# Turning TensorE's partial rows with a 0/1 matrix instead of the identity, in a two-layer hybrid block on one core

## The reference, cut to what matters

```
silu_c, silu_cc = silu(c), silu(c_ctx)
for l in range(2):
    mod_l = (silu_c @ ada_w[l] + ada_b[l]).reshape(6, 1024)     # ada_w[l] is 1024 x 6144
    mod_c = (silu_cc @ ada_w[l] + ada_b[l]).reshape(6, 1024)
    sh1, sc1, g1, sh2, sc2, g2 = mod                            # for each of the two streams
    h = rmsnorm(x, norm_mix_g[l]) * (1 + sc1) + sh1
    y = mixer(h)                   # l = 0: RG-LRU and a 31-tap convolution; l = 1: attention
    x = x + g1 * y
    h = rmsnorm(x, norm_ffn_g[l]) * (1 + sc2) + sh2
    scores = sigmoid(h @ router_w)                              # router_w is 1024 x 16
    sel = scores + router_bias     # best group of 4 experts, then the top 2 inside it
    x = x + g2 * (sum over the chosen experts of gate * expert(h))
return rmsnorm(x_latent, final_norm_g)
```

## Time and profile before

| | |
|---|---|
| runs (3) | 1002.47 us median, 1002.4 to 1004.44 |
| the profiled execution | 1001.4 us |
| its span in the profile | 999.6 us |
| TensorE busy | 906.7 us, 91% of the span |
| TensorE weight loads | 473.6 us |
| VectorE busy | 379.8 us, 38% |
| ScalarE busy | 255.3 us, 26% |
| GpSimd busy | 112.9 us, 11% |
| read from and written to HBM | 314 GB/s over the span |

### The profile page before, as it was taken

One profiled execution on the slowest core, in us unless ns is written; L12 is line 12 of the kernel. 1 busy time (PEld: TensorE's weight loads), 2 busy tenths in 40 slices (PEclk: granted clock), 3 DMA queues, 4 the chain that ended last, 5 costly groups with the idle time before them and its releaser, 6 DMA issues.

```text
span 999.6 us, 14180 instructions
## 1 busy us (share of the span) xinstructions
PE 906.7 (91%) x5142; PEld 473.6 (47%) x5143; DVE 379.8 (38%) x815; ACT 255.3 (26%) x393; POOL 112.9 (11%) x220
## 2 busy tenths in 40 slices
PE   3899999999689999999999869999959999998786
PEld 1433343444346655665656434467424455554443
DVE  1389989833542222222222261774351111111012
ACT  3423446412312111112211230264121111111112
POOL 2300000100021111111111210000003111111010
PEclk9999999999989999999999969999978999999999
DMA  9992595756699899999999983971577999999994
GB/s 352 348 350 84 200 340 217 275 210 253 242 376 330 324 396 379 399 395 396 396 395 400 360 292 128 368 284 49 205 263 252 379 389 395 391 396 392 395 391 191
DMA packets 133652, 314.32 MB, mean 314 GB/s; under 512 B 4516, under 2 KB 4884, under 8 KB 133616
## 3 DMA queue, kind: packets, MB, share of 16 engines
q1 hardware_dynamic: 120144, 275.78, 74.5%
q0 software_dynamic: 8800, 29.75, 8.2%
q10 hardware_dynamic: 4672, 8.30, 2.3%
HBM read 299.35 MB, written 14.47 MB: 314 GB/s over the span
## 4 chain that ended last, share of the span: by engine, by line
PE 61%; DMA 27%; DVE 6%; ACT 3%; issue 2%; POOL 0%; ACTq 0%; SPq 0%; DVEq 0%; POOLq 0%
PE ps L757 17%; PE ps L770 9%; PE ps L559 8%; PE ps L595 6%; DMA weight_ring<-in_exp_w_up 6%; DMA weight_ring<-in_exp_w_down 5%; DMA weight_ring<-in_exp_w_gate 4%; PE ps L828 3%; PE ps L488 3%; PE ps L870 3%; DMA arena<-in_exp_w_up 2%; DMA hT<-in_exp_w_down 2%; DMA arena<-in_exp_w_gate 2%; DMA weight_ring<-in_ev_w_in 2%; DVE arena L1059 2%
## 5 line engine op out<-in xcount | busy, mean ns | idle before, releaser
L757 PE MATMUL ps<-weight_ring,arena 128*64 128x256 f32 x1792 | 201.4, 382 | 10.7 <-DMA weight_ring<-in_exp_w_up 5.6
L757 PEld LDWEIGHTS ps<-weight_ring,arena 128*64 128x64 f32 x1792 | 140.5, 138 | 79.0 <-issue 19.6
L1330 DVE TENSOR_TENSOR arena<-arena,ps 128x128 f32<-128x128 f32 x78 | 18.9, 284 | 269.0 <-PE ps L757 269.0
L559 PE MATMUL ps<-hT,weight_ring 128*128 128x512 f32 x256 | 113.6, 597 | 1.1 <-DMA weight_ring<-in_ev_w_in 0.6
L770 PE MATMUL ps<-weight_ring,arena 128*64 128x512 f32 x448 | 102.3, 597 | 2.5 <-DVE arena L1343 0.2
L1059 DVE SCALAR_TENSOR_TENSOR arena<-arena,par 128x512 f32<-128x512 f32 x132 | 95.0, 749 | 5.3 <-PE ps L559 1.2
L757 PE MATMUL ps<-arena 128*64 128x256 f32 x704 | 80.1, 385 | 5.1 <-DMA arena<-in_exp_w_up 4.8
L1713 ACT ACT_TABLE_LOAD x39 | 50.0, 1283 | 129.5 <-issue 129.2
L559 PEld LDWEIGHTS ps<-hT,weight_ring 128*128 128x128 f32 x256 | 47.4, 190 | 64.4 <-issue 63.0
L757 PEld LDWEIGHTS ps<-arena 128*64 128x64 f32 x704 | 56.6, 139 | 31.5 <-issue 6.1
L595 PE MATMUL ps<-weight_ring,arena 128*128 128x512 f32 x160 | 70.8, 595 | 0.7 <-DVE arena L1480 0.5
(11 more groups left out here) (315 smaller groups left out, 906.1 us busy)
## 6 DMA issues: line engine op xcount, KB each, us to landing
weight_ring<-in_ada_w SPq DMA_DIRECT2D x24, 2048.0 KB, 12.7
weight_ring<-in_exp_w_gate SPq DMA_DIRECT2D x22, 2048.0 KB, 10.8
weight_ring<-in_exp_w_up SPq DMA_DIRECT2D x22, 2048.0 KB, 12.0
weight_ring<-in_exp_w_down SPq DMA_DIRECT2D x22, 2048.0 KB, 11.8
arena<-in_exp_w_gate SPq DMA_DIRECT2D x10, 2048.0 KB, 11.2
hT<-in_exp_w_down SPq DMA_DIRECT2D x10, 2048.0 KB, 11.8
arena<-in_exp_w_up SPq DMA_DIRECT2D x10, 2048.0 KB, 12.0
weight_ring<-in_ev_w_in SPq DMA_DIRECT2D x4, 2048.0 KB, 19.2
```

The source lines that it names most:

```text
L559: last = mm(ps[:, m % 4, :], wide(slot)[:, k, P * j:P * j + P], hT[:, k, :], start=(k == 0), stop=(k == KD - 1))
L757: last = mm(ps[64 * fh:64 * fh + 64, bank, 0:256], xgT[:, k % 4, 64 * (k // 4):64 * (k // 4) + 64], w[:, k, 256 * fh:256 * fh + 256], star ...
```

## The change

The turn is no longer a transpose. The partial tile stays the stationary operand, but what moves past it is `sel`: the product of the turned tile with `sel` adds the four partial rows at once. For the modulation two columns of `sel` are used, for the router 16. VectorE's reduction of a chunk becomes an addition of the bias while it is read from PSUM, and the later `add_bias` is gone; the waits that it held stay. The router's reduction is gone, and ScalarE's sigmoid reads the logits from PSUM.

```diff
-        s_ls = sem("logits_summed")
...
 def ada_columns(bank=7):
...
                 for i in range(4):
-                    last = tr(ps[:, bank, P * i:P * i + P], ada_part[:, n % 2, P * i:P * i + P], ident[:, :])
+                    last = mm(ps[:, bank, 2 * i:2 * i + 2], ada_part[:, n % 2, P * i:P * i + P], sel[:, 0:2], start=True, stop=True)
                 last.then_inc(s_col, 1)
...
 def logits(i0, i1, count):
...
                     for i in range(i0, i1):
-                        last = tr(ps[:, 7, P * i:P * i + P], ada_part[:, 0, P * i:P * i + P], ident[:, :])
+                        last = mm(ps[:, 7, E * i:E * i + E], ada_part[:, 0, P * i:P * i + P], sel[:, :], start=True, stop=True)
                     last.then_inc(s_lg[l], 1)
...
 def sum_columns(count, bank=7):
...
-                    v.tensor_reduce(mods[:, l, 4 * c:4 * c + 4, :],
-                                    ps[:, bank, :].rearrange("p (i g m) -> p i m g", i=4, g=4)[:, :, 0:2, :], AX,
-                                    ALU.add).then_inc(s_red, 1)
-
-            def add_bias(l, c0, c1):
-
-                dve.wait_ge(s_red, ada[0])
-                w = mods[:, l, 4 * c0:4 * c1, :]
-                b0 = C_ADAB + 48 * l
-                return v.tensor_tensor(w, w, par[:, b0 + 4 * c0:b0 + 4 * c1].unsqueeze(2).to_broadcast([P, 4 * (c1 - c0), 2]),
-                                       ALU.add)
+                    b0 = C_ADAB + 48 * l + 4 * c
+                    v.tensor_tensor(mods[:, l, 4 * c:4 * c + 4, :], ps[:, bank, 0:8].rearrange("p (i m) -> p i m", i=4),
+                                    par[:, b0:b0 + 4].unsqueeze(2).to_broadcast([P, 4, 2]), ALU.add).then_inc(s_red, 1)
 
             sum_columns(4)
-            link(add_bias(0, 0, 4))
+            dve.wait_ge(s_red, ada[0])
...
                     if ada[0] == 10:
-                        link(add_bias(0, 4, 10))
+                        dve.wait_ge(s_red, ada[0])
...
-                dve.wait_ge(s_lg[l], 2)
-                v.tensor_reduce(logit_sb(l).rearrange("p (t e) -> p t e", t=n),
-                                ps[:, 7, 0:P * n].rearrange("p (t g m) -> p t m g", t=n, g=4)[:, :, 0:E, :], AX,
-                                ALU.add).then_inc(s_ls, 1)
                 dve.wait_ge(s_sc, l + 1)
...
-                act.wait_ge(s_ls, l + 1)
-                s.activation(score_sb(l), logit_sb(l), ACT.Sigmoid).then_inc(s_sc, 1)
+                act.wait_ge(s_lg[l], 2)
+                s.activation(score_sb(l), ps[:, 7, 0:E * n], ACT.Sigmoid).then_inc(s_sc, 1)
```

More of the change, by code:

```diff
@@ L337, in score_sb @@
             return rt(l, (848, 984)[l], 64)[:, 0:E * len(toks(l))]
-        def logit_sb(l):
-            return rt(l, (912, 1048)[l], 64)[:, 0:E * len(toks(l))]
         OH_GATE = 3600
@@ L1179, in _ @@
             add_residual(0, range(NT), lambda t: 0 if cond_of(t) == CON else 1, after_residual)
-            link(add_bias(0, 10, 12))
+            dve.wait_ge(s_red, ada[0])
             dve.sem_inc(s_mods, 1)
@@ L1298, in route @@
                     sum_columns(1, 3)
-                    link(add_bias(1, 10, 12))
+                    dve.wait_ge(s_red, ada[0])
                     dve.sem_inc(s_mods, 1)
@@ L1311, in route @@
                     sum_columns(1, 3)
-                    link(add_bias(1, 0, 6))
+                    dve.wait_ge(s_red, ada[0])
                     dve.sem_inc(s_mods, 1)
@@ L1388, in _ @@
                     sum_columns(1)
-            link(add_bias(1, 6, 10))
+            dve.wait_ge(s_red, ada[0])
             link(gain(mods[:, 1, 8 * SC2:8 * SC2 + 8, :], 1, SC2, C_FFNG + 8))
```

## The result

The change makes the kernel slower: 1016.26 us (median of 6 runs, 1011.49 to 1018.05) against 1002.43 (6 runs, 1000.59 to 1004.44) beside it, a ratio of 1.0132 [1.0117, 1.0147]. The profiled execution took 1017.79, its span is 1016.0, 16.4 more than before.

What follows compares the result with a forecast made beforehand. It took TensorE (61% of the chain) and transfers (27%) as the bound. Terms 0.9 + 2.4 + 1.7 - 0.44 + 0.65 - 0.36 + 0.1 = +4.95 us on 1002.47 gave 1007.4, range 1004.2 to 1010.3.

Steps and rivals of the forecast that it cites:

- The turn: Each chunk's turn on TensorE: eight passes taking 0.86 instead of 0.43, so +0.43 us each.
- L704's step: 0.107 us between float32 passes at L704, with 34 moving columns; taken to hold for the turn's 2 columns.
- Small passes are cheap: Rival: passes step on after 0.027, a turn saves 0.21, -3.3 in all, 999.2 us; chance 8%.
- Passes don't overlap: Rival: each pass waits for the one before, +1.8 a turn on some 14 turns, +25, 1027 us; chance 3%.
- Head stage: From 52.9 to 192: longer turns ahead of the steps VectorE waits for, +2.4 us.
- output projection: Up to 258: four longer turns on a TensorE queue that nothing else holds up, +1.7 us.
- projection between the MoEs: Two turns in the projection count, two fall in TensorE's gap before the expert rows; +0.65 us.
- Start: Up to 52.9: four longer turns in series make L559 1.4 to 1.8 late, +0.9 us after waiting time there.
- the transfer at 52.9: Awaited weight chunk that stays in place; 0.57 of waiting and about 0.17 of drain there cover part of the start's delay.
- First and second router: Sigmoid reads PSUM and starts earlier, -0.44 and -0.36 us; a late turn in the second adds +0.1.
- just inside that wait: First router: two turns growing by 0.85 and 0.43 fit the first MoE tile's 1.21 wait; otherwise the gain is lost.
- TensorE slows down: Rival: nearly empty passes in full-rate stretches bring on 1.2 GHz; one or two falls of 1.9, 1009.3 to 1011.2; chance 10%.

Runs made afterwards that it cites:

- head_out_new: Kernel before, with the new turns only for chunks 4 to 14 (head stage and output projection); 1006.26 us, ratio 1.0054 to before.
- start_ident_product: Kernel before, with the first four turns as float32 products with the 128-column identity, eight passes each; 1003.60 us, ratio 1.0013 to before.
- start_new: Kernel before, with only the first four chunks turned and summed the new way; 1009.82 us, ratio 1.0072 to before.
- route_turns_new: Kernel before, with the new turns only for chunks 15, 16, 17, 22 and 23, beside the routers; 1004.18 us, ratio 1.0021 to before.
- router_light: Kernel before, with the new router logits and 24 unused identity transposes at one wait of each router; 1001.28 us, ratio 0.9987 to before.
- kept_busy: Changed kernel, with 28, 6 and 6 unused identity transposes behind the first three modulation products; 1009.14 us, ratio 1.0072 to before.
- start_old: Changed kernel, with the first four chunks turned and summed as before; 1010.34 us, ratio 1.0077 to before.
- all_filled: Changed kernel, with unused identity transposes behind the first three modulation products and at waits in both routers; 1009.62 us, ratio 1.0080 to before.
- start_twice: Kernel before, with each transpose of the first four turns made twice, 128 columns per pass; 1003.62 us, ratio 1.0021 to before.

## Why the prediction was right and wrong

The direction was right, the size was not: 1007.4 was forecast, 1004.2 to 1010.3 the range, 1016.26 measured.

**The turn: right.** L704's step held for 2 columns: 0.88 between the turn's start and the next product, 192 matmul records, as forecast. *Small passes are cheap* and *Passes don't overlap* are both out. The Trainium skill's rule for a matmul of 1 to 64 columns ("TensorE: Matmul & The Clock Gate", "Back-to-back issue gap") has no support in these float32 passes: at the full rate eight take 0.88, 0.11 each. The same page's weight load of 107 ns for 128 columns ("LDWEIGHTS (loading the stationary operand)") agrees with that; at the lower rate, at 21.89, eight take 1.80, 0.22 each.

**Head stage, output projection, projection between the MoEs: right.** +2.19, +1.71 and +0.85 against 2.4, 1.7 and 0.65; head_out_new alone shows the first two again. VectorE stood where it was said to: it waits for TensorE at 173.92 too, ahead of the scan that lay at 164.03 before. VectorE of after:

```profile
173.92 0.69 DVE L1096 TENSOR_TENSOR arena<-arena 128x512 f32<-128x512 f32 x1 [0.67 <-PE ps L555]
```

**Start: the step that failed.** It said "TensorE may reach its full pace sooner for having been at work longer, so 0.4 to 0.85". The opposite happened. I counted a turn of twice the passes as more work, where its passes move 2 columns: TensorE kept the lower rate from 23.69 to the run of transposes at 35.92 and beyond. From start to start, its 7.07 are these: two products at 3.64 where one of 2.94 and one of 1.92 stood (2.4); the first three turns, 1.80, 1.80 and 1.72 instead of 1.04, 0.59 and 0.49 (3.2); the 24 transposes, 4.17 instead of 2.78 (1.4). The expected length of the turns, tried alone in start_ident_product, was right at 1.5. The rate's part pushed the head stage past the transfer at 52.9, so that the wait there covered only about 0.8 of it: in start_new the three steps take 20.8, against 21.6 before, and the chunk behind them starts 7.2 late. In after they take 22.5, 1.7 more than in start_new, with a fall of the granted clock that start_new hasn't; so 7.93 behind the third step, where 0.9 was forecast, and 1.7 of it isn't the change's for certain. Busy time of after from 40 to 50 (columns as in the earlier trace rows), granted clock 0.83:

```profile
40.00:50.00 10.00, 8.63 (x40) 4.25 (x40) 4.79 (x14) 6.27 (x12) 5.48 (x9) 0.83 0.82 262
```

**First and second router: one size wrong, the rest open.** The sigmoid gained 0.18 and 0.26, not 0.44 and 0.36. In after's trace the cover, "just inside that wait", didn't hold: the product behind the logits' turn takes 3.64 (1.92 before, at 268.84), the write of `mod_rows` and with it GpSimd's gather follow later, and the first tile comes 1.79 later instead of 0.44 earlier. TensorE and GpSimd of after:

```profile
280.95 3.64 PE L484 MATMUL ps<-weight_ring,cond 128*32 128x512 f32 x16
...
285.80 0.60 POOL L1886 DMA_DIRECT2D mod_rows<-arena  x1 [8.50 <-ACT arena L1618]
...
294.91 1.06 POOL L1899 DMA_INDIRECT arena<-h_rows,gidx  x1 [0.30 <-issue]
...
302.69 1.11 PE L711 MATMUL ps<-ident,arena 128*128 128x128 f32 x4 [0.99 <-DMA arena<-h_rows,gidx]
```

Before the change GpSimd still waited 1.95 for VectorE ahead of the gather; now it waits for nothing. That is how the two traces differ, and not shown to be the change: the same product takes 3.64 with the old turns as well, and the unchanged router of head_out_new takes 34.21 where after takes 34.28. What is measured is route_turns_new's 1.2 to 2.1; how it comes about stays open. The 1.15 that the second router gives back, 0.26 of it forecast, is no gain of the change for certain either: 0.86 of it is one group of eight products that holds the queue for 0.97 instead of 1.83 (L686 at 761.35, L690 at 747.43 before), and it is 0.97 in router_light too and 1.83 in kept_busy.

***TensorE slows down*: the right kind of rival, at the wrong place.** I looked for a fall inside a full queue, and there is none (1.92 behind a turn in the output projection). The loss is where the queue was never full: TensorE doesn't fall there, it fails to rise. I gave it 10% and one or two falls of 1.9; of the 5.5 to 7.2 at the start the longer turns themselves are 1.5 and the rate is the rest.

**The sum of the parts.** Start 5.5 to 7.2, head stage and output projection 4.0 (5.4 by the ratio), turns at the routers 2.1 (1.2 by the medians), projection 0.85, logits -0.5: 12 to 15 (11 with the smaller number for the routers), and 13.8 was measured, 13.2 by the ratio. The intervals of the parts are 3 to 5 us wide, so the agreement is weak evidence. **Open:** the last 2.14 of the profiled execution, where the last up products take 5.36 instead of 3.67. This is also in the traces of start_old and all_filled and not in those of start_new and kept_busy; the execution lies 1.5 above its median, and I can't say how much of it belongs to the change.

## What to carry to other kernels

Before trading one kind of TensorE pass for another, ask what the pass does for the rate of what comes behind it, not only what it costs: in this kernel's chain of small steps, passes of 128 columns kept 6 us that passes of 2 columns lost, at nearly the same length. A float32 product against a 128x128 stationary operand took two passes of 0.11 with 34 columns and with 2, a float32 transpose one. Before a stage's loss in one trace is put down to a change, look at the same stage in a trace whose code there is unchanged: it moved by 1.7 here. And work put into a wait must be shorter than the wait at the rate that it will itself have there, which the 18 fillers ahead of the first tile were not.

## What the runs showed of the hardware

- Eight 2-column passes per turn, between products of 16 passes and waits for ScalarE, left TensorE at 1.2 GHz from 23.69 to past 35.92 in after; the same number of 128-column passes had it at 2.4 GHz by 27.72 as products (start_ident_product) and by 27.84 as transposes (start_twice). In kept_busy 28 transposes of the identity took 3.28 us, 0.117 each, where at the lower rate all_filled's 18 took 0.206 each.
- The granted clock stands at 1.00 while passes take twice as long (start_new, 25 to 30). A clock row is a witness against the full rate when it is below 1.00, and none for it at 1.00.
- The first MoE tile took 7.13 in all_filled, behind fillers that ran up to its own transposes; it took 9.33 in router_light, behind 2.47 of waiting, although TensorE had the full rate 10 us earlier.
- The rate differs between executions where the code is the same: the product behind the first router's logits took 1.92 in before and 3.4 to 3.6 in the other twelve traces, and that router 32.49 in before and 33.14 to 34.22 in four kernels that leave it as it was.
